# A two-layer encoder on one core: 28 of the first tile's 128 expert dot products go from VectorE to TensorE

## The reference, cut to what matters

```python
def peer_ffn(xn, w_query, sub_keys, u, v):
    q = (xn @ w_query).reshape(b, s, 8, 2, 128)
    sc = jnp.einsum('bshpc,hpnc->bshpn', q, sub_keys)      # 128 keys in each half
    s_top, i_top = lax.top_k(sc, 16)
    cand = (s_top[..., 0, :, None] + s_top[..., 1, None, :])   # 16 x 16
    cand_idx = i_top[..., 0, :, None] * 128 + i_top[..., 1, None, :]
    best, pos = lax.top_k(cand, 16)
    expert = take_along_axis(cand_idx, pos)                # 8 heads x 16 = 128 slots for a token
    gate = softmax(best)
    act = gelu(einsum('tkd,td->tk', u[expert], xn))
    return einsum('tk,tkd->td', gate * act, v[expert])
```

## Time and profile before

| | us |
|---|---|
| median of three runs | 3182.01 (3176.41 to 3183.42) |
| the profiled execution's own time | 3178.66 |
| its span, first to last instruction | 3176.9 |
| layer 0, first tile's dots | 530.1 to 960.2 |
| layer 0, second tile's dots | 960.2 to 1279.2 |
| layer 1, first tile's dots | 1889.2 to 2309.7 |
| layer 1, second tile's dots | 2309.7 to 2628.4 |
| mean granted TensorE clock | 0.789 of full |

### The profile page before, as it was taken

One profiled execution on the slowest core, in us unless ns is written; L12 is line 12 of the kernel. 1 busy time (PEld: TensorE's weight loads), 2 busy tenths in 40 slices (PEclk: granted clock), 3 DMA queues, 4 the chain that ended last, 5 costly groups with the idle time before them and its releaser, 6 DMA issues.

```text
span 3176.9 us, 20155 instructions
## 1 busy us (share of the span) xinstructions
PE 1954.3 (62%) x6560; PEld 1383.5 (44%) x6560; DVE 2289.4 (72%) x3263; ACT 543.1 (17%) x1421; POOL 1020.9 (32%) x1028
## 2 busy tenths in 40 slices
PE   8999998452203410899999575422034108999994
PEld 4685644442202300666666345422023006666662
DVE  1341113999999999866666749999999998666667
ACT  1241110100008920300000001000089203000000
POOL 0000001323234333254444413232343332444444
PEclk9999999776655555899999788766555559999997
DMA  5323254879889999699999948797899996999998
GB/s 214 148 106 138 100 200 164 356 316 384 308 362 422 421 422 422 213 405 409 409 409 409 379 203 366 313 387 305 362 421 421 422 422 216 407 409 409 409 409 330
DMA packets 194504, 1058.71 MB, mean 333 GB/s; under 512 B 21856, under 2 KB 22240, under 8 KB 121312
## 3 DMA queue, kind: packets, MB, share of 16 engines
q0 software_dynamic: 147456, 805.37, 63.2%
q1 hardware_dynamic: 46944, 252.06, 20.2%
HBM read 1055.24 MB, written 2.10 MB: 333 GB/s over the span
## 4 chain that ended last, share of the span: by engine, by line
DMA 44%; DVE 30%; PE 21%; issue 2%; POOL 2%; ACT 1%; another core or an unknown queue 0%; DVEq 0%; SPq 0%; POOLq 0%
DMA arena<-pu,idx_all 19%; DVE arena L1061 17%; DMA arena<-pvg,idx_all 15%; DMA xnT<-pvg,idx_all 9%; PE bank L1221 6%; DVE h L1078 3%; PE bank L1306 3%; PE bank L1504 2%; PE bank L1512 2%; PE low L1426 2%; PE low L1415 1%; PE low L1484 1%; PE bank L1415 1%; PE bank L1462 1%; DVE arena L1030 1%
## 5 line engine op out<-in xcount | busy, mean ns | idle before, releaser
L1061 DVE CUSTOM_DVE_ANT_0 arena<-arena,low 128x2048 f32<-128x2048 f32 x476 | 1075.1, 2285 | 55.9 <-DMA arena<-pu,idx_all 54.3
L415 POOL DMA_INDIRECT arena<-pu,idx_all x512 | 516.2, 1008 | 1553.7 <-DVE cst L1061 784.6
L1521 PE MATMUL low<-arena 128*128 128x512 f32 x2048 | 879.6, 592 | 0.7 <-DMA arena<-pvd 0.7
L1521 PEld LDWEIGHTS low<-arena 128*128 128x128 f32 x2048 | 604.7, 295 | 275.4 <-DMA arena<-pvd 1.4
L1078 DVE SCALAR_TENSOR_TENSOR h<-arena,cst,h 128x1024 f32<-128x1024 f32 x240 | 308.0, 1286 | 164.2 <-DMA arena<-pvg,idx_all 156.8
L1078 DVE SCALAR_TENSOR_TENSOR h<-xnT,cst,h 128x1024 f32<-128x1024 f32 x240 | 307.6, 1285 | 160.2 <-DMA xnT<-pvg,idx_all 150.9
L430 POOL DMA_INDIRECT arena<-pvg,idx_all x256 | 252.9, 988 | 298.5 <-DVE h L1078 218.8
L430 POOL DMA_INDIRECT xnT<-pvg,idx_all x256 | 251.6, 983 | 281.0 <-DVE h L1078 217.2
L1493 PE MATMUL bank<-cst,arena 128*128 128x128 f32 x8 | 2.8, 448 | 514.3 <-DVE cst L1067 514.3
L1504 PE MATMUL bank<-arena 128*128 128x128 f32 x512 | 132.8, 441 | 201.6 <-ACT arena L678 201.6
L1462 PE MATMUL bank<-xnT,arena 128*128 128x256 f32 (+1 forms) x1280 | 239.2, 350 | 17.1 <-DMA arena<-wq 13.5
(11 more groups left out here) (207 smaller groups left out, 1838.2 us busy)
## 6 DMA issues: line engine op xcount, KB each, us to landing
arena<-pvd SPq DMA_DIRECT2D x256, 512.0 KB
arena<-w_proj SPq DMA_DIRECT2D x22, 2048.0 KB, 8.1
arena<-wq SPq DMA_DIRECT2D x16, 2048.0 KB, 12.0
arena<-w_out SPq DMA_DIRECT2D x9, 2048.0 KB, 8.1
arena<-pu,idx_all POOLq DMA_INDIRECT x512
gB<-gains SPq DMA_DIRECT2D x5, 1024.0 KB, 10.2
xnT<-pvg,idx_all POOLq DMA_INDIRECT x256
arena<-pvg,idx_all POOLq DMA_INDIRECT x256
```

Of the source, the lines that this page charges most:

```text
L415: nc.gpsimd.indirect_dma_start(U[n // HK][n % UR], None, pu[L], bass.IndirectOffsetOnAxis(idx_all[:, g, k:k + 1], 0)).then_inc(u_got[n % U ...
L1061: vec.tensor_tensor_reduce(out=u, in0=u, in1=low[:, :] if staged else xns[t], scale=1.0, scalar=0.0, op0=ALU.mult, op1=ALU.add, accum_out= ...
L1521: ins = mm(psum[2 * t + c][:, 0:VH], W[t][:, :, n], vdense[:, n % DR, c * VH:(c + 1) * VH], start=n == 0, stop=n == NK - 1)
```

## The change

28 slots of the first tile, k = 2, 6, 10 and 14 of groups 1 to 7, are dotted by TensorE. They are gathered into two buffers of their own (`UX`). For each, TensorE transposes the 16 pieces of 128 x 128 (four at a time into bank 4), ScalarE copies each four to SBUF (`turn_u`), TensorE multiplies the 16 transposed pieces with the transposed tokens and sums them in bank 5; the result has in row e, column t the product of token e's expert row with token t, so that its diagonal is wanted. VectorE takes it with a product with the identity, summed along the row (`pick`, 128 x 128), four slots at a time, one group later behind k = 3. The second buffer pair of the transposed data (`UXT`) and the junk output of `pick` lie where ScalarE's one-hots of the second tile lie later.

The other 100 slots have a ring of six buffers in the first tile, the second tile keeps a ring of seven, in new places. Query weights have two buffers: head 2 shares with heads 0, 4 and 6, and its load waits for the queries of head 0 on the second tile. On TensorE two turned slots stand ahead of each head's queries and two behind its scores; on ScalarE the copies stand around `route_exp` and `route_q`. The gather of the third slot of the second tile (d = 2) waits until all 28 are multiplied. The weighing of the first tile moves from k = 1 to k = 5 of group 8.

```diff
-UR = 7
+UT0, UT1, UP = 6, 7, 2
-        shared = ring(0, 4) + [fifth]
-        U = [shared + ring(W_AT + KC * S, 2), shared + ring(W_AT + P * P, 2)]
+        U = [ring(0, UT0), ring(W_AT + P * P, 2) + [fifth] + ring(0, 4)]
+        UX = ring(UT0 * D, UP)
+        UXT = [a.rearrange("p (c n) -> p c n", c=KC) for a in ring(OUT_AT + D, 2)]
-        wq_slots = [wqb[:, 0], wqb[:, 1], wqb2]
+        wq_slots = [wqb[:, 0], wqb[:, 1]]
+        def on_pe(n):
+            return PK <= n < HK and n % 4 == 2
+        dots = [n for n in range(ROWS) if not on_pe(n)]
+        turns = [n for n in range(ROWS) if on_pe(n)]
...
             for L in range(LAYERS):
-                if L == 0:
-                    sp.wait_ge(s["out_mm"], TB * NO)
-                    load_wq(0, 2)
-                for hd in range(3, PH):
-                    sp.wait_ge(s["q_mm"], EVENTS * L + (3 if hd == 4 else hd + 1))
+                for hd in range(2, PH):
+                    sp.wait_ge(s["q_mm"], EVENTS * L + hd + 1)
                     load_wq(L, hd)
...
             def gather_u(L, n):
+                if n % PK == 0:
+                    pool.wait_ge(s["idx_ready"], L * EVENTS + event(n // HK, n // PK % PH) + 1)
+                if on_pe(n):
+                    i = turns.index(n)
+                    if i >= UP:
+                        pool.wait_ge(s["ux_tp"], 4 * (L * NUX + i - UP + 1))
+                    elif L == 0:
+                        pool.wait_ge(s["out_mm"], TB * NO)
+                    nc.gpsimd.indirect_dma_start(
+                        UX[i % UP], None, pu[L], bass.IndirectOffsetOnAxis(row(n), 0)).then_inc(ux_got[i % UP], 16)
+                    return
...
+                    if d >= UT0:
+                        pool.wait_ge(s["dot_done"], L * NDOT + d - UT0 + 1)
...
+                elif d >= UT1:
+                    pool.wait_ge(s["dot_done"], L * NDOT + ND0 + d - UT1 + 1)
+                elif d >= 3:
+                    pool.wait_ge(s["dot_done"], L * NDOT + max(i for i in range(ND0) if i % UT0 == d - 3) + 1)
+                elif d == 2:
+                    pool.wait_ge(s["ux_mm"], (L + 1) * NUX)
...
+            def turn_u(L, i):
+                if i >= 2:
+                    e.wait_ge(s["ux_mm"], L * NUX + i - 1)
+                for b in range(4):
+                    e.wait_ge(s["ux_tp"], 4 * (L * NUX + i) + b + 1)
+                    activation(UXT[i % 2][:, 4 * b:4 * b + 4], psum[4][:, :].rearrange("p (a b) -> p a b", a=4),
+                               ACT.Copy).then_inc(s["ux_ev"], 1)
...
+                for j in range(1, PH):
+                    turn_u(L, 4 * j - 4)
+                    turn_u(L, 4 * j - 3)
+                    if j + 3 < EVENTS:
+                        route_exp(L, j + 3, 0, 2)
+                    if j + 4 < EVENTS:
+                        route_q(L, j + 4, 0, 2)
+                    turn_u(L, 4 * j - 2)
+                    turn_u(L, 4 * j - 1)
...
+            def pick(L, i):
+                n = turns[i]
+                if i >= 4:
+                    v.wait_ge(s["picked"], L * NUX + i // 4 * 4)
+                v.wait_ge(s["ux_mm"], L * NUX + i // 4 * 4 + 4)
+                vec.tensor_tensor_reduce(out=picked[:, i % 4], in0=psum[5][:, i % 4 * P:(i % 4 + 1) * P], in1=ident, scale=1.0, scalar=0.0,
+                                         op0=ALU.mult, op1=ALU.add, accum_out=act[:, 0, n:n + 1]).then_inc(s["picked"], 1)
...
-                        dot(L, j * PK + k)
+                        if not on_pe(j * PK + k):
+                            dot(L, j * PK + k)
+                        if 2 <= j <= PH and k == 3:
+                            for i in range(4 * j - 8, 4 * j - 4):
+                                pick(L, i)
...
+            def dot_u(L, i):
+                pe.wait_ge(ux_got[i % UP], 16 * ((L * NUX + i) // UP + 1))
+                g = 4 * (L * NUX + i)
+                def multiply(b):
+                    pe.wait_ge(s["ux_ev"], g + b + 1)
+                    for c in range(4 * b, 4 * b + 4):
+                        ins = mm(psum[5][:, i % 4 * P:(i % 4 + 1) * P], UXT[i % 2][:, c], xnT[:, c, 0:P], start=c == 0, stop=c == KC - 1)
+                    return ins
+                for b in range(4):
+                    if g + b:
+                        pe.wait_ge(s["ux_ev"], g + b)
+                    for x in range(4):
+                        ins = tr(psum[4][:, x * P:(x + 1) * P], UX[i % UP][:, (4 * b + x) * P:(4 * b + x + 1) * P], ident)
+                    ins.then_inc(s["ux_tp"], 1)
+                    if b == 0 and i >= 4:
+                        pe.wait_ge(s["picked"], L * NUX + i // 4 * 4)
+                    if b:
+                        multiply(b - 1)
+                multiply(3).then_inc(s["ux_mm"], 1)
...
+                for j in range(1, PH):
+                    dot_u(L, 4 * j - 4)
+                    dot_u(L, 4 * j - 3)
+                    if j + 4 < EVENTS:
+                        queries(L, j + 2, j % 2, j + 4, 0, 2)
+                        scores(L, j + 2, j + 4, 0, 2)
+                    dot_u(L, 4 * j - 2)
+                    dot_u(L, 4 * j - 1)
```

More of the change, by code:

```diff
@@ L321, in load_wq @@
             def load_wq(L, hd):
-                slot = 2 if hd == 2 else hd % 2
+                slot = hd % 2
                 sp.dma_start(wq_slots[slot].rearrange("p k c -> p (k c)"), wq[L, hd]).then_inc(ld_wq[slot], 16)
@@ L1453, in queries @@
                 n0 = EVENTS * L + ev_
[L1455 to L1457 removed]
+                slot = par
+                pe.wait_ge(ld_wq[slot], 16 * (4 * L + hd // 2 + 1))
                 if n0:
```

79 lines of the change are left out of this document (42 added, 37 removed).

## The result

The kernel after took 3154.06 us (median of four runs, 3152.77 to 3158.11), the one before 3182.72 beside it. The ratio is 0.992, with a 95% interval of 0.9908 to 0.9933: faster, and by 29 us where 60 were predicted. The profiled execution took 3154.75 us with a span of 3153.0, against 3178.66 and 3176.9 before, so 23.9 us of span are to be found.

A forecast was written before the change was run, and what follows sets the result against it. VectorE was taken to bound each layer's U stage until the last routing block, gathers behind it. 42.6 - 5.0 - 5.6 - 1.8 + 2 - 4.5 gave 27.7 us a layer; two layers plus 4.7 gave 60.1: 3122 us, forecast 3105 to 3142, range 3090 to 3168.

The forecast's parts named there:

- What bounds the kernel: U stage: VectorE bounds until group 6's last routing block, 50.7 us a group; behind it gathers bound at 416 GB/s.
- Dots taken off and picks added: VectorE before the last routing block: 22 dots of 2.21 us less, twenty picks more; 42.6 us a layer gained.
- A turned slot on TensorE: Transposes, copies and products of one slot: 5.0 us to the last transposes, 6.5 to the product; half clock 10 and 11.5.
- What is late next: Groups 3 to 6: late gathers make a group 43.9 us, 45.8 with a query weight load; 1.8 and 5.6 given back.
- Groups 1 and 2: Gathers of slots 26 and 34 wait for TensorE's transposes; 7.0 of 12 us gained, 5 a layer given back.
- Two query weight buffers: Layer 0 start: head 2's load no longer runs beside gather 4, gaining 4.7 us (0 to 5.0); later load costs 0.
- Ring of six and two: Eight buffers look one row further ahead; behind the last routing block this gives 2 us a layer back (0 to 4).
- The hand-over: Start of second tile: gather d = 2 waits for slot 126's product; 2.2 or 7.2 us lost, 4.5 taken a layer.
- The clock: TensorE in groups 1 to 5: full clock, 2.4 GHz, since its work runs in stretches of 7 to 27 us.
- half clock in part: Rival: one turned slot, ahead of queries or behind scores, at 1.2 GHz; loop about 49 us, 3159 us; chance 0.18.
- All hidden: Rival: no gather is late, so VectorE's 42.6 us a layer come through whole; 89.5 us gained, 3092 us; chance 0.10.
- Slower: Rival: GpSimd, TensorE, ScalarE loop sets the pace, 68 us at half clock against 50.7; 3240 at half the time; chance 0.12.

The follow-up runs named there:

- experiment 8: Kernel after with 14 turned slots instead of 28 (k = 2 and 10 of each group), picks in pairs: 3129.49 us, ratio 0.9851.
- experiment 10: Kernel after with three turned slots a group (k = 2, 6 and 10; 21 in all) and picks behind k = 1: 3121.93 us, ratio 0.9825.
- experiment 1: Kernel after with ScalarE copying the four results from bank 5 to SBUF; TensorE waits for that copy, not VectorE's picks: 3143.14 us, ratio 0.988.
- experiment 2: Kernel after with the four picks behind k = 1 of a group instead of k = 3: 3144.65 us, ratio 0.989.
- experiment 7: Kernel after without the query weight loads of heads 6 and 7, which changes the output: 3143.57 us, ratio 0.9898.
- experiment 13: Kernel after with 24 turned slots (none in group 1), picks behind k = 1, and the products' wait moved to d = 6: 3125.82 us, ratio 0.9836.
- experiment 5: Kernel after with picks behind k = 1 and the second tile's fifth shared buffer last in its ring: 3135.84 us, ratio 0.9875.
- experiment 12: Kernel after without turned slots in group 1, 24 in all from group 2 on: 3142.15 us, ratio 0.988.
- experiment 6: Kernel after with picks behind k = 1, fifth shared buffer last in the second tile's ring, and slot 18 ahead of head 2's queries: 3156.1 us, ratio 0.9938.
- experiment 4: Kernel before with two query weight buffers instead of three, nothing else of the change: 3175.99 us, ratio 0.9988.
- experiment 11: Kernel after without any turned slot, keeping two query weight buffers, the ring of six and the second tile's ring: 3185.01 us, ratio 1.0018.
- experiment 3: Kernel after with the second tile's fifth shared buffer last in the ring, moving the products' wait from d = 2 to d = 6: 3142.34 us, ratio 0.9878.

## Why the prediction was wrong in size, step by step

**What bounds the kernel.** Right. The gain came where the first regime was, and behind the last route block there was nothing to gain: C did not get shorter in any kernel by more than 1.1 us.

**Dots taken off and picks added.** Right. 456 dots are left. A pick takes 0.285 us, and since the next starts 0.21 behind it, it costs VectorE 0.21 where 0.30 was taken; experiments 8 and 10 land on VectorE's own sum to 0.1 us.

**A turned slot on TensorE.** 6.6 to 7.4 us for each, where 6.5 was taken: slot k = 6 from 731.17 to the queries at 738.62 is 7.4.

**What is late next: the step that failed.** It counted the dots, gathers, products, queries and transposes, and gave a ring of 43.9 us for a group (its items for VectorE add up to 44.1, which changes nothing). It left out one wait of the diff, the one with which TensorE waits before the first product of a group until VectorE has picked the four results of the group before from bank 5. The step had VectorE wait for its dot k = 3 and pick behind it, and had TensorE ready by then; it never asked who waits for the picks. So GpSimd's late gather holds VectorE, VectorE's picks hold TensorE, and TensorE's transposes hold GpSimd: 48.1 us in the trace of group 3. In both layers B took 191.7 us instead of 179.4: the groups with a load 49.1 us on average where 45.8 were forecast, those without 46.8 where 43.9 were. That is 12.3 missing in each layer, 25 of the 39 us that the layers fell short.

Experiments 1 and 2 open the ring by two different edits and give back 6 of the 12 in the layers (3 in layer 1 of the first), and 12.7 and 9.5 us by the ratios. So the picks are shown to be about half of the miss in B. The other half has no single cause shown. With the picks out of the way, TensorE waits for its own gathers (12.7 us in the window of experiment 2), which is the loop that the step did count; it runs at 45.0 to 45.6 us where 43.9 were forecast. By experiment 7 a load costs about what was forecast, but in experiment 13 the groups with one took 47.5 us on average and those without 44.6, so some part may still be its. B also differed by 2 to 5 us between kernels with the same code in it (experiments 2 and 5, 12 and after). With three slots a group the rest goes away where there is no load (experiment 10). No run gave the turned slots a third buffer, which would be the direct test of that loop.

**Groups 1 and 2.** Mis-sized. A gained 8.2 and 2.9 us, or 7.2 with the first dot's delay, where 11.7 and 7.0 were forecast. In layer 0 the route block of group 2 ended at 701.8, and the step's own working had 701.9; the 4.7 us of the weight load, which the sum put on top, did not come on top. In layer 1, where no such gain was in the sum, the 4 us that are missing stay open. Slot 26 was issued at 634.19, before the 636.2 of the forecast. Yet taking the slots of group 1 away made the kernel faster by 12 us, 7 of them in A (experiment 12): a turned slot at a place where TensorE is still busy with the second tile's queries costs more than a dot on VectorE. How much of the miss is this hold and how much the late load of head 2 stays open; experiment 6 was to tell and moved another wait instead.

**Two query weight buffers.** Right by themselves: 4.8 us by the medians where 4.7 was forecast, with an interval of 1 to 7, so the tenth is luck (experiment 4). In the change dot 4 came earlier too (550.18), but the end of group 2 did not for that, as said above.

**Ring of six and two.** Wrong. It was taken to cost nothing in the first tile and to give 2 us behind it. Without turned slots the new buffers cost 9.5 us (experiment 11): some 6 in B, and C was 369.5 / 369.4, 2 us a layer longer and not shorter. With turned slots the two at the side carry one slot in four, and with half the slots C was as before, so the 9.5 can't simply be added to the sum.

**The hand-over.** The mechanism was right and the size too small. Slot 126 landed at 935.2 and its product ended at 943.6, 8.3 us instead of 6.5 at full clock; the clock was 0.79 from 935 to 950 us. The gather behind it was issued at 943.83, and dot 130 came 8.2 us after the one before it, instead of 2.5. C was 5.0 and 5.9 us longer than before, and the net forecast of it was 2.5. What the step did not see is that the order of the ring alone made this gather early (experiment 3).

**The clock.** Right for most of the time, and with it the rival *half clock in part* fell in its size. TensorE was granted 0.94 and 0.96 in the windows above. But over the 3.5 us behind each wait for the picks, of 3.6 to 4.7 us in layer 0, the granted clock was 0.50 to 0.69, so mostly 1.2 GHz. The last 36 us of each stretch were granted 1.00, 2.4 GHz. The rows behind the wait that ended at 724.53:

```profile
724.50:728.00 3.50, 3.47 (x19) 3.47 (x20) 3.50 (x3) 0.96 (x2) 0.00 (x0) 0.60 1.00 424
728.00:768.00 40.00, 35.36 (x243) 32.34 (x242) 35.61 (x82) 8.82 (x16) 12.33 (x14) 0.99 0.94 381
```

The rest of slot k = 2 took 6.6 us from 724.53 to 731.17, where the same part of slot k = 10 took 5.0. So by these rows a wait for the picks costs some 1.6 us beyond itself, an estimate. TensorE: Matmul & The Clock Gate, in the Trainium skill (HAM oscillation), has waits between short bursts return the engine to 1.2 GHz every time. This trace agrees behind each wait, though the wait was for VectorE. It isn't the page's case otherwise, since the stretches between the waits were 43 to 45 us long and the window as a whole stayed at 0.96.

**The other rivals.** *All hidden* fell with the first kernel: VectorE waited 63.4 us for gathers from 530 to 960 us, 22.9 before. *Slower* is the one whose shape was nearest: a loop through several engines did set the pace, but at 48 us and nearly full clock, below the 50.7 from which it decides. Its fourth member was VectorE and not the clock.

## What to carry to other kernels

When work moves to an idle engine, write down for every wait of the diff who waits and for whom, also for the ones that only protect a result buffer; if the list closes, add up the whole ring, because no busy share will show it. Then try less of the change before more: here half the slots were worth 47 us, three quarters 59 (with the earlier picks, beside which all of them are worth 36) and all of them 29, because the part that is still cheap is that in which the old bound stays the bound. The order of buffers in a ring at the seam of two stages is free to choose and was worth 6 us a layer beside all 28 slots, and nothing beside half of them.

## What the runs showed of the hardware beyond that

A reduced product of 128 x 128 from a PSUM bank takes VectorE 0.285 us, and the next starts 0.21 us behind it, less than a tenth of the 2.29 us dot of 2048 columns. A group of four fp32 transposes takes 0.60 us at full clock and up to 1.1 behind a wait (1.12 us behind the wait of 13.42 in experiment 6). GpSimd's issue of a gather took 0.94 us while VectorE read one operand from PSUM; it took 1.97 us at 943.83 in the kernel after, and 3.02 and 1.77 us in that of experiment 3, each beside a dot whose two operands both lie in SBUF. Of the 512 issues in the kernel after, 28 fell beside such a dot, and 23 of these took over 1.2 us and up to 3.02; of the other 484 only two did, at 1.24 us the longest. The two were only seen side by side; no run changed the one alone. SBUF — State Buffer, in the Trainium skill (SBUF: two separate sides), says that VectorE in a mode that takes the port pair it shares with GpSimd keeps GpSimd from writing the descriptors of its transfers until the instruction ends. These rows would fit that; that the dot runs in such a mode is shown by no run here.
